# Output projections, down matrices and residual turned token-major in a fused two-model transformer kernel

## The reference

```python
# first_block, twice
h = rms_norm(x, g_pre_mix[l]);  m = hybrid_mixer(h, ...)       # ends: y @ w_out, 1024 x 1024
x = x + rms_norm(m, g_post_mix[l])
h = rms_norm(x, g_pre_ffn[l]);  f = conv_ffn(h, ...)           # ends: (gelu(gate) * up) @ w_down, 2816 x 1024
x = x + rms_norm(f, g_post_ffn[l])
# second_block, once: ffn1 (swiglu, 0.5 * norm), a mixer that ends in merged @ w_out, ffn2 (as ffn1)
def rms_norm(x, gain):
    return x * lax.rsqrt(jnp.mean(x * x, axis=-1, keepdims=True) + RMS_EPS) * gain
```

## Time and profile before

| what | value |
|---|---|
| median of 3 runs | 3128.06 us (3123.47 to 3134.88) |
| profiled execution: own time | 3122.07 us |
| its span, first to last instruction | 3120.3 us |
| mean granted TensorE clock | 0.975 |
| PE busy | 2915.7 us (93%) |
| ACT, POOL, DVE busy | 1287.7, 1222.2, 1130.2 us |
| units of weights | 251 |

### The profile page before, as it was taken

How to read it: one execution, slowest core, us unless ns; L and a number is a source line. 1 busy time by engine, 2 the same in 40 slices (tenths; PEclk the granted TensorE clock), 3 DMA queues, 4 the chain that set the end, 5 groups by cost and what they waited for, 6 DMA issues and landing times.

```text
span 3120.3 us, 40469 instructions
## 1 busy us (share of the span) xinstructions
PE 2915.7 (93%) x14437; PEld 2280.1 (73%) x14437; DVE 1130.2 (36%) x1501; ACT 1287.7 (41%) x1707; POOL 1222.2 (39%) x308
## 2 busy tenths in 40 slices
PE   7998998999989989998999989999498999999998
PEld 5864686888768755886887868887296778778886
DVE  5154213555122362125553044430204531344422
ACT  5356443555335365434554233332224353333332
POOL 2410254344554200544444644455331325444454
PEclk9999999999999999999999999999699999999998
DMA  6310132233335100332332333322221213323322
GB/s 142 91 32 1 41 107 81 81 94 87 92 91 111 55 2 1 95 107 68 94 98 83 101 77 95 100 82 76 76 85 34 71 37 95 94 81 94 97 86 73
DMA packets 441757, 242.35 MB, mean 78 GB/s; under 512 B 39158, under 2 KB 440246, under 8 KB 441654
## 3 DMA queue, kind: packets, MB, share of 16 engines
q1 hardware_dynamic: 438320, 240.13, 27.9%
q10 hardware_dynamic: 3334, 0.85, 0.2%
HBM read 238.48 MB, written 2.70 MB: 77 GB/s over the span
## 4 chain that ended last, share of the span: by engine, by line
PE 84%; issue 4%; ACT 4%; DVE 4%; POOL 1%; SPq 1%; DVEq 1%; DMA 0%; ACTq 0%; POOLq 0%
PE pair L1531 56%; PE pair L1546 6%; PE pair L1547 6%; PE pair L1551 6%; PE pair L1603 2%; PE pair L1722 1%; PE pair L1743 1%; POOL wlo L455 1%; SPq L406 1%; PE pair L1760 1%; PE pair L1802 1%; DVE nstat L1227 1%; PE pair L1800 1%; DVE sL L1275 0%; ACT tmp L743 0%
## 5 line engine op out<-in xcount | busy, mean ns | idle before, releaser
L455 POOL TENSOR_TENSOR wlo<-raw,whi 128x2048 fp32r<-128x2048 f32 x251 | 1155.8, 4605 | 1775.0 <-ACT whi L515 1775.0
L515 ACT ACTIVATE whi<-raw 128x2048 fp32r<-128x2048 f32 x251 | 480.1, 1913 | 502.2 <-PE pair L1531 452.9
L1531 PE MATMUL pair<-hh,whi 128*128 128x512 f32 (+1 forms) x1504 | 587.0, 390 | 3.8 <-POOL wlo L455 2.4
L1531 PE MATMUL pair<-hl,whi 128*128 128x512 f32 (+1 forms) x1504 | 585.6, 389 | 0.0
L1531 PE MATMUL pair<-hh,wlo 128*128 128x512 f32 (+1 forms) x1504 | 585.5, 389 | 0.0
L1531 PEld LDWEIGHTS pair<-hh,whi 128*128 128x128 f32 (+1 forms) x1504 | 281.0, 187 | 68.6 <-issue 7.6
L1531 PEld LDWEIGHTS pair<-hh,wlo 128*128 128x128 f32 (+1 forms) x1504 | 280.9, 187 | 60.3
L1531 PEld LDWEIGHTS pair<-hl,whi 128*128 128x128 f32 (+1 forms) x1504 | 281.0, 187 | 60.0
L1546 PE MATMUL pair<-hh,whi 128*128 128x512 f32 x752 | 296.0, 394 | 26.2 <-ACT hh L550 17.7
L1547 PE MATMUL pair<-hh,wlo 128*128 128x512 f32 x752 | 295.0, 392 | 0.0
L1551 PE MATMUL pair<-hl,whi 128*128 128x512 f32 x752 | 233.5, 392 | 0.0
(11 more groups left out here) (333 smaller groups left out, 4225.5 us busy)
## 6 DMA issues: line engine op xcount, KB each, us to landing
raw<-in_w_in SPq DMA_DIRECT2D x122, 512.0 KB, 4.1
raw<-in_w_up SPq DMA_DIRECT2D x88, 512.0 KB, 4.6
raw<-in_ffn_w_gate SPq DMA_DIRECT2D x44, 512.0 KB, 4.0
raw<-in_ffn_w_up SPq DMA_DIRECT2D x44, 512.0 KB, 5.2
raw<-in_w_out SPq DMA_DIRECT2D x24, 512.0 KB, 4.4
raw<-in_w_down SPq DMA_DIRECT2D x32, 384.0 KB, 3.6
raw<-in_ffn_w_down SPq DMA_DIRECT2D x32, 384.0 KB, 3.6
raw<-in_w_down SPq DMA_DIRECT2D x32, 320.0 KB, 4.0
```

What stands on the lines that cost most here:

```text
L455: pool.tensor_tensor(wlo[:, s, :], raw[:, s, :], whi[:, s, :].bitcast(f32), ALU.subtract).then_inc(lo_ready, 1)
L515: act.activation(whi[:, s, :], raw[:, s, :], ACT.Copy).then_inc(hi_ready, 1)
L1531: o = pe.matmul(out, l, r, start=start and first, stop=stop and last)
```

## The change

The residual and the outputs of the seven branches become token-major: [128 partitions = tokens of one tile i, tile i of 4, 1024 features].

- **Branch outputs** (`by_tokens`): the activations are the stationary operand (`swap=True`), the moving one is 512 columns of weights. A down unit holds 4 or 3 tiles of rows by 512 columns (DOWN_PARTS), so a down matrix takes 12 units instead of 16 and a pass over columns 0 to 511 goes before that over 512 to 1023. The units fall from 251 to 235; the number of matmuls in these products stays (192 for an output projection, 528 for a down matrix).
- **Norms**: the mean of squares is a sum along the free axis, which ACT accumulates while it squares (`accum_out`); Ln and Exp are of 128 x 1. DVE multiplies the branch by its gain in PSUM (`gained`) and adds root times branch to x (`added`). The sums on PE (`variance`, `variance_of_x`) go.
- **Turning back** (`turn`): POOL forms x * gain (`scaled`), DVE a diagonal matrix of the roots (`diagonal`), and PE multiplies the two, eight 128 x 128 products for each token tile, which transposes and norms at once. ACT and DVE split the result into `hh` and `hl` a token tile at a time.
- **Start and end**: x is loaded straight into its place, the first weights before it; the output is stored from `x` without transposes or `ostage`. The gains are rows broadcast to 128 partitions, one load of 512 KB for each norm.
- The first unit after a norm is no longer treated apart; `h_tiles` waits for the last token tile.

```diff
-        x = keep("x", [P, KT, T])
+        x = keep("x", [P, TT, D])
-CONST_COLS, ... ("strict01", P), ...      # cst: 3560 bytes
+CONST_COLS, ...                           # cst: 3048 bytes
-        gains = keep("gains", [P, GAINS * KT])
+        diag = keep("diag", [P, 2, P])
+        sums = keep("sums", [P, CH, TT])
+        halfsum = keep("halfsum", [P, TT])
+        root1 = keep("root1", [P, TT])
+        root2 = keep("root2", [P, TT])
...
+DOWN_PARTS = ((0, 4), (4, 8), (8, 12), (12, 15), (15, 18), (18, 22))
...
 # PE
+            def by_tokens(v, s0, parts, b, inp, ready):
+                n = len(parts)
+                for j in range(2 * n):
+                    c, (k0, k1) = j // n, parts[j % n]
+                    vv, s = at_unit(v, s0, j)
+                    opened(vv, s)
+                    if c == 0:
+                        ready(k1 - 1)
+                    for i in range(TT):
+                        for k in range(k0, k1):
+                            wt = [w[s][:, (k - k0) * 512:(k - k0 + 1) * 512] for w in (wh, wl)]
+                            o = three(bank[4 * c + held(s0, i)][:, :], wt, [t[:, k, i * P:(i + 1) * P] for t in inp],
+                                      k == 0, k == parts[-1][1] - 1, swap=True)
+            def turn(m, xg, s0):
+                for i in range(TT):
+                    pe.wait_ge(S.diag_set, 4 * m + i + 1)
+                    for h in range(CH):
+                        pe.wait_ge(S.xg_ready, 8 * m + 2 * i + h + 1)
+                        for k in range(4):
+                            at = h * 512 + k * P
+                            o = pe.matmul(bank[4 * h + held(s0, i)][:, k * P:(k + 1) * P], xg[:, i % XG, at:at + P], diag[:, i % 2], start=True, stop=True)
-                down(v0 + 27, 0, a1hi, a1lo, FT * (l + 1))
-                variance(4 * l + 3)
-                variance_of_x(4 * l + 4)
+                by_tokens(v0 + 27, 0, DOWN_PARTS, 2 * l + 1, (a1hi, a1lo), act_tiles(FT * l))
+                turn(2 * l + 2, xg_d, 0)
...
 # POOL
+            def scaled(m, xg, gq):
+                pool.wait_ge(S.gq_in, 16 * (m + 1))
+                for i in range(TT):
+                    ...
+                    for h in range(CH):
+                        cols = slice(h * 512, (h + 1) * 512)
+                        pool.tensor_tensor(xg[:, i % XG, cols], x[:, i, cols], gq[:, cols], ALU.mult).then_inc(S.xg_ready, 1)
...
 # ACT, end of by_tokens
+                    if j < 2 * n - 1 and not (last and j == 2 * n - 2):
+                        upper(vv + 1, s)
...
+                    post_root(vv, s, b, 0, s0)
+                    post_root(vv, s, b, 1, s0)
+                    pre_root(m, 0)
+                    post_root(vv, s, b, 2, s0)
+                    pre_root(m, 1)
+                    post_root(vv, s, b, 3, s0)
+                    pre_root(m, 2)
+                    pre_upper(m, 0, s0)
+                    pre_root(m, 3)
+                    pre_upper(m, 1, s0)
+                    pre_upper(m, 2, s0)
+                    pre_upper(m, 3, s0)
                     upper(vv + 1, s)
...
 # DVE, end of by_tokens
+                for i in range(TT):
+                    gained(1, i)
+                    dve.drain()
+                    added(i)
+                    if i > 0 and not last:
+                        diagonal(m, i - 1)
```

More of the change, by code:

```diff
@@ L394, in _ @@
                         unit(v0 + 16 + i, s, twin(A["w_up"][l], (2 * i + s) * P, A["w_up"][l], (2 * i + s) * P + FF, s))
-                with sp.Fori(0, KT) as m:
-                    for s in range(2):
-                        unit(v0 + 27 + m, s, half_rows(A["w_down"][l], m, s, s))
+                down(v0 + 27, 0, A["w_down"][l], A["g_post_ffn"][l], gq_d,
+                     A["g_pre_mix"][l + 1] if l + 1 < DEPTH else A["ffn1_pre_g_2"][0])
             v2 = DEPTH * VL
@@ L490, in _, with rest_of @@
[L490 to L505 removed]
+            def rest_of(first, end):
+                if first % 2:
+                    rest(first // 2, 1)
+                    first += 1
+                n = (end - first) // 2
+                if n:
+                    with pool.Fori(0, n) as i:
+                        for s in range(2):
+                            rest(first // 2 + i, s)
+                if end % 2:
+                    rest(end // 2, 0)
@@ L545, in pre_upper @@
-            def pre_upper(m, between=None):
-                for k in range(KT):
-                    if k == KT // 2 and between is not None:
-                        between()
-                    act.wait_ge(S.h_set, KT * m + k + 1)
-                    act.activation(hh[:, k], tmp[:, k // 2 % 2] if k % 2 and between is None else NORM[(k if between is not None else k // 2) % 2][:, :], ACT.Copy).then_inc(S.hh_ready, 1)
-            def pre_norm(n, m):
-                pre_squares(n, m)
-                pre_upper(m)
@@ L556, in down @@
-            def down(v, s0, n):
-                def two_outputs(i, last):
-                    for q in range(2):
-                        for half in range(2):
-                            vv, s = v + 2 * i + (s0 + 2 * q + half) // 2, (s0 + half) % 2
-                            tile(vv, s, 1)
-                            if half == 1:
-                                act.wait_ge(S.sq_used, KT * n + 2 * i + q - 1)
-                                act.activation(sq[:, q], bank[2 * q][:, :], ACT.Square).then_inc(S.sq_done, 1)
-                                if last and q == 1:
-                                    root(n)
-                            upper(vv + 1, s)
-                with act.Fori(0, KT // 2 - 1) as i:
-                    two_outputs(i, False)
-                two_outputs(KT // 2 - 1, True)
@@ L574, in out_proj @@
[L574 to L583 removed]
+                token_done(v, s, b, 1, i)
```

624 lines of the change are left out of this document (263 added, 361 removed).

## The result

| | before | changed |
|---|---|---|
| median | 3127.19 us (4 runs, 3123.47 to 3134.88) | 3083.51 us (4 runs, 3081.49 to 3085.68) |
| ratio | | 0.9857, 95% interval 0.9837 to 0.9877 |
| profiled execution, its span | 3122.07, 3120.3 us | 3083.70, 3081.9 us |
| mean granted clock | 0.975 | 0.983 |

The changed kernel is 43.7 us faster, where 21 were forecast. In the profiled executions the difference is 38.4.

The account below looks back on a forecast made before the run. PE, busy 93% of the span, was taken to bound the kernel. From 3122.1 us, -62.5 (boundaries, clock, start, end, down front), +46 (h spacing) and -4 (down and output products) gave 3101.6, with 6 for the median 3107; range 3048 to 3125.

Parts of the forecast that it names:

- five boundaries: Stretches without products of the reference, behind projections or down matrices: 12 us each, 60 instead of 100.3 together, -40.
- clock at restarts: Matmuls after each of seven boundaries lose 3 us to a lower granted clock, against 1 now: +13, bounds 0 and +20.
- behind ffn1: Boundary after ffn1: ACT still waits for a load behind the tables, then 18.5 us of work; 57 instead of 62.6, -5.
- start: Kernel start until the first product of h: 26 us instead of 35.4, POOL's chain longest; -9, bounds -6 and -12.
- end: After the last matmul: one branch root, gain, additions and a store, 6.4 us instead of 23.4; -17.
- front of the down matrices: PE's wait for the hidden layer: a down unit first needs 4 hidden tiles, not 11 and then 22; -4.5 us.
- spacing of h: 6,768 matmuls with h moving go from 226.7 to 233.5 ns as hh moves 192 bytes off a multiple; +46 us.
- down and output products: Weights now move in these matmuls: between -13 and +5 us by operand places, taken as -4.
- case 1: Boundaries shorten and the matmuls of h space out: 3107 us, its own range 3090 to 3125, chance 0.5.
- a multiple of 512: Matmuls are short where the operand begins an exact multiple of 512 bytes behind whi: 226.7 ns, against 233.5 to 234.8 off it.
- The median: 6 us added to the sum, as the profiled execution of before lay 6 below the median of three runs.
- Cases 2, 3 and 4: 2: spacing of h stays, 3061 (0.36); 3: spacing grows, 3152 at 240 ns (0.09); 4: boundaries don't shorten, 3148 (0.05).

Follow-up runs that it names:

- The pad kernels: Unused bytes alone added: changed kernel plus 320 bytes ahead of hh, 3030.91 us; kernel before plus 192 ahead of hh, 3172.97, or ahead of x, 3125.42.
- the sweep: Kernel body replaced by 36 blocks of 96 matmuls, operand distance stepped by 32 bytes: a block takes 22.06 us at 0, 22.27 at 64, 22.77 at 160.
- the pad of 64 bytes: Changed kernel with 64 unused bytes, so hh begins 256 bytes beyond a multiple of 512 behind whi: 3033.22 us.
- the two experiments on rests: Changed kernel with 320 pad bytes, PE's rest put ahead of the turning products: 3058.66 us; or lengthened right ahead of h by three ACT squares: 3063.64 us.
- the first experiment's kernel: Changed kernel with 320 unused bytes ahead of hh, putting hh a multiple of 512 bytes behind whi: 3030.91 us, ratio 0.9683 to before.
- the all-aligned changed kernel: Changed kernel with 320 and another 96 unused bytes, so all large operands begin a multiple of 512 behind whi: 3020.77 us, ratio 0.9656.

## Why the prediction was wrong, and where it was right

The sign and the mechanism were right, the size was not: the time lies within the range of 3048 to 3125, but 23.5 us below the 3107 forecast, and the gain is twice the 21 us that were forecast. By the forecast's own terms, with what the profiled executions show:

| term | forecast | measured | from |
|---|---|---|---|
| five boundaries | -40 | -47.8 | 52.53 against 100.30 |
| clock at restarts | +13 | -4.8 | below |
| behind ffn1 | -5 | -6.5 | 56.08 against 62.60 |
| start | -9 | -6.9 | 28.28 against 35.16 |
| end | -17 | -17.5 | 5.91 against 23.40 |
| front of the down matrices | -4.5 | -4.5 | that wait is gone |
| spacing of h | +46 | +44.6 | below |
| other products of the mixers | 0 | +6.1 | below |
| down and output products | -4 | -1.4 | their stages, without the front waits |
| sum | -20.5 | -38.7 | the executions differ by 38.4 |

**The layout was right,** and with it case 1: the spacing of h rose from 226.8 to 233.4 ns (233.5 forecast). The four up stages take 7.0 us more each, 27.9 together. The mixers are 22.6 us longer net (1306.09 us in three windows before, 1328.71 after); their restarts lost 1.7 us before (start) and 1.5 after (second boundary), which leaves 22.8. Of these, by start-to-start times, 16.7 are the mixers' 2,544 matmuls of h with 512 columns, so that the forecast's 6,768 cost 44.6 us. The other 6.1 are in products that the forecast put at nothing: 2.3 in the value projections, 3.8 mostly in small products of the mixers. Their cause was not sought. The pad kernels show the place of h as cause, not only as company. What was wrong is the rule as put, "a multiple of 512": the sweep says 256, and the difference moving less still. That it gave the right number for h was in part luck, for at 256 beyond a multiple it would have failed, as the pad of 64 bytes shows. By the sweep's rule a1 and y stay at distance 160, y2 goes from 128 to 64 and a2 from 0 to 64, and the down and output products could have been read as nearly unchanged. The rule of the Trainium skill that the prediction set against the trace ("TensorE: Matmul & The Clock Gate", section "Step-by-step: what each phase is for": loading weights takes nothing from the running matmul) would make the places of the two operands indifferent, and this does not hold here. The sweep's blocks, with nothing but matmuls and weight loads, take from 22.06 to 22.77 us by the distance of their operands alone.

**The step that failed is the clock,** "I let each of seven restarts lose 3 us, against 1 now: +13" (by these figures it is +14). This was the costliest single boundary of one trace taken for all. In four traces of before-like kernels the first 48 matmuls behind 24 boundaries lost 1.6 to 2.9 us at six and nothing at eighteen, and at each of four starts 1.6 to 2.1; in the profiled execution of before it was 1.7 + 2.9 + 1.6 = 6.2 us. In the changed kernel one of seven lost 1.5 us, hence -4.8 rather than +13, 18 us of the miss. In eight traces of it and its variants with the same short rest or one ahead of the turning products, five of 48 boundaries lost 1.5 or 1.6, each time the second. The second is also the one with the longest rest: PE's idle time right ahead of h is 1.7 to 2.6 us there and 0.6 to 1.3 at the other 40, none of which lost anything. The forecast took few matmuls and small pieces for a clock that falls. The rows of the profile say 0.99 to 1.00, and the two experiments on rests say what matters: how long PE has rested right before the long run. The turning products fill that place, and at five of six boundaries of the changed kernel 1.0 to 1.2 us of rest is left. Why one such rest of 2 to 3 us costs something and another does not stays open.

**The boundary** was a term mis-sized, 10.5 us for 12: the handovers of ACT's chain are at most 0.35 us apiece, most of them 0.15 or less, and Ln and Exp of 128 x 1 took 0.29 and 0.20, about as bounded. That ACT's interleaved order is the path was right (14.7 us without it).

**The median** was another 6 us. The forecast added what the profiled execution of before lay below its median. The changed kernel's profiled execution, 3083.70, lies on its own. Restarts that lose now and then may be why before scatters over 11.4 us and the changed kernel over 4.2; that was not tried.

**Behind ffn1, end, start, down front** came close to what was worked out, the start 2 us short of its term. Cases 2, 3 and 4 did not happen; case 2 is the first experiment's kernel, for which the forecast said 3061; it took 3031, some 18 of the difference by the clock, 6 by the median and 8 by the boundaries, less 2 at the start.

Of the signs that the prediction named, the first `hh` came 10.8 us behind the last `yhi` (12 said), ACT's wait for raw was 53.7 (near 50), the first product at 28.3 (26), the end 5.9 (6.4), and 48 matmuls of h took 11.27 (11.2 for case 1). The clock below 0.75 in the windows is the one that did not show.

## What to carry to other kernels

Before a change that adds or drops small tensors is judged, look at where the large matmul operands come to lie: here 192 bytes cost 50 us, more than the change gained net, and pads that put the moving and the still operand a multiple of 256 bytes apart gave it back. A term read off the one worst place of a single trace is no price for all places; count how many of the like places show it. And where a chain behind a boundary stands on a load, look at what SP has queued ahead of that load: the loads of three units moved past 65 others gave 41 us.

## What was not expected of the hardware

The same stream of 512-column float32 products, with PE never waiting and the clock at 1.00, runs at 226.8 to 235 ns each by the distance of its operands modulo 256 bytes. The dependence is there with all other engines still, too. What in the memory makes it so was not found. The kernel before's a2 products, with tokens moving, took 228.9 ns at distance 0; the all-aligned changed kernel's, with weights moving, take 226.7. That stays open too. A turning product, float32 and 128 x 128, is two records 0.112 us apart (16 records for the eight products of a token tile, in 1.95 to 2.05 us), so 0.22 us each. That is the 0.225 us that the prediction read from the transposes at the kernel's start, each of which is one record.
